# Token row loads on GpSimd, a tile's expert choice beside the context units, a buffer for the context, two gates ahead

## What is computed

```python
def peer_ffn(u, wq, k1, k2, eu, ev):              # for each chunk of 128 tokens
    q = (xc @ wq).reshape(PEER_CHUNK, PEER_HEADS, 2, half)
    v1, i1 = lax.top_k(s1, PEER_TOPK)             # s1, s2: scores against 2 x 128 keys per head
    v2, i2 = lax.top_k(s2, PEER_TOPK)
    cand = (v1[..., :, None] + v2[..., None, :]).reshape(PEER_CHUNK, PEER_HEADS, -1)
    top_s, pos = lax.top_k(cand, PEER_TOPK)
    g = jax.nn.softmax(top_s, -1)
    h = jax.nn.gelu(jnp.einsum('thkd,td->thk', eu[eidx], xc), approximate=False)
    return jnp.einsum('thk,thkd->td', g * h, ev[eidx])
```

## Time and profile before

| | before |
|---|---|
| median of 3 runs | 3122.6 us |
| profiled execution | 3111.5 us (span 3109.7 us) |
| busy: TensorE matmul | 2384.4 us, 77% |
| busy: VectorE | 1922.8 us, 62% |
| busy: ScalarE | 408.3 us, 13% |
| busy: GpSimd | 732.5 us, 24% |
| moved | 1029.87 MB, mean 331 GB/s |
| mean granted clock of TensorE | 0.786 |

### The profile page before, as it was taken

The page is one execution under the profiler, slowest core; times in us unless marked ns, Lnnn a source line. Parts: engine busy times, 40 slices in busy tenths (PEclk is TensorE's granted clock), DMA queues, the critical chain, the costliest instruction groups (busy, mean ns, idle before and its releaser), DMA issues.

```text
span 3109.7 us, 34657 instructions
## 1 busy us (share of the span) xinstructions
PE 2384.4 (77%) x11936; PEld 1287.6 (41%) x11936; DVE 1922.8 (62%) x6212; ACT 408.3 (13%) x1015; POOL 732.5 (24%) x779
## 2 busy tenths in 40 slices
PE   6989996597899968758878877676897656665555
PEld 5878892053456535324545542112786111121111
DVE  3689977757545465877754455554448855555555
ACT  2151120014200010012010010000421000000000
POOL 0000002332322222222222223331001333333332
PEclk8999996597899979768989986556998555566556
DMA  8618748798899989868999999998144989999997
GB/s 322 237 68 333 296 173 331 301 402 346 341 403 418 393 320 381 337 263 355 378 374 408 421 376 407 397 395 353 53 152 155 351 335 397 392 378 403 399 398 304
DMA packets 155376, 1029.87 MB, mean 331 GB/s; under 512 B 19136, under 2 KB 29888, under 8 KB 34496
## 3 DMA queue, kind: packets, MB, share of 16 engines
q0 software_dynamic: 110592, 805.36, 64.9%
q1 hardware_dynamic: 31648, 209.70, 17.3%
q10 hardware_dynamic: 12960, 12.59, 1.2%
HBM read 1018.66 MB, written 8.91 MB: 330 GB/s over the span
## 4 chain that ended last, share of the span: by engine, by line
PE 45%; DMA 26%; DVE 15%; POOL 5%; issue 4%; ACT 3%; ACTq 1%; SPq 0%; DVEq 0%; POOLq 0%
DMA ring<-in_peer_uv,eT 24%; PE PS L1233 12%; DVE ring L2253 7%; PE PS L901 6%; POOL ring L717 5%; PE PS L1252 4%; PE PS L817 4%; PE PS L998 4%; PE PS L971 2%; PE PS L908 2%; PE PS L1079 2%; PE PS L819 1%; PE PS L1170 1%; PE PS L928 1%; PE PS L1095 1%
## 5 line engine op out<-in xcount | busy, mean ns | idle before, releaser
L2253 DVE CUSTOM_DVE_ANT_0 ring<-ring,PS 128x512 f32<-128x512 f32 x1536 | 994.0, 684 | 831.9 <-PE PS L1252 491.8
L717 POOL DMA_INDIRECT ring<-in_peer_uv,eT x768 | 730.6, 951 | 2348.0 <-PE PS L1233 1431.4
L1252 PE MATMUL PS<-xr,onesb 3*128 3x512 bf16 x1536 | 548.1, 482 | 485.5 <-DVE hcol L2253 400.7
L1233 PE MATMUL PS<-ring,zcol 128*32 128x512 f32 x3072 | 573.5, 886 | 108.4 <-DVE zcol L2263 106.4
L1252 PEld LDWEIGHTS PS<-xr,onesb 3*128 3x128 bf16 x1536 | 108.1, 95 | 1049.9 <-DVE hcol L2253 569.9
L1233 PEld LDWEIGHTS PS<-ring,zcol 128*32 128x32 f32 x3072 | 102.6, 141 | 390.2 <-issue 213.7
L901 PE MATMUL PS<-uT,W 128*128 128x256 f32 x1024 | 245.2, 388 | 3.7 <-ACT mix L1373 3.7
L1623 ACT ACTIVATE ge<-hdot 128x4 f32<-128x4 f32 x192 | 39.5, 206 | 1435.4 <-DVE hdot L2258 1435.3
L901 PEld LDWEIGHTS PS<-uT,W 128*128 128x128 f32 x1024 | 190.3, 191 | 53.3 <-issue 24.0
L1696 DVE CUSTOM_DVE_ANT_0 ring<-ring 128x1024 f32<-128x1024 f32 x160 | 190.1, 1220 | 7.6 <-DMA ring<-in_w_rows 3.4
L817 PE MATMUL PS<-uT,W 128*128 128x256 f32 (+1 forms) x720 | 168.7, 388 | 17.8 <-ACT uT L1316 17.8
(11 more groups left out here) (289 smaller groups left out, 2156.6 us busy)
## 6 DMA issues: line engine op xcount, KB each, us to landing
ring<-in_w_rows SPq DMA_DIRECT2D x40, 1024.0 KB, 7.9
W<-in_w_in SPq DMA_DIRECT2D x30, 1024.0 KB, 9.3
W<-in_w_gate SPq DMA_DIRECT2D x16, 1408.0 KB, 8.0
W<-in_w_gate SPq DMA_DIRECT2D x16, 1280.0 KB, 8.9
W<-in_w_out SPq DMA_DIRECT2D x20, 1024.0 KB, 5.1
W<-in_w_gate SPq DMA_DIRECT2D x16, 1152.0 KB, 10.5
ring<-in_w_q SPq DMA_DIRECT2D x16, 1024.0 KB, 13.4
ring<-in_peer_uv,eT POOLq DMA_INDIRECT x768, 10.3
```

Source lines behind the costliest of these rows:

```text
L717: pool.indirect_dma_start(ring[:, slot, :], None, (peer_uv0, peer_uv1)[b.l], bass.IndirectOffsetOnAxis(eT[:, f % 2, t:t + 1], 0)).then_inc ...
L1233: last = T.matmul(PS[k * NR:(k + 1) * NR, (6 + h) * 512:(7 + h) * 512], zcol[:, g % 2, k, NR - 1 - at:2 * NR - 1 - at], ring[:, slot, D + ...
L1252: T.matmul(bank(x_bank(q, n) + h), onesb[p0:p0 + 3, :], xr[p0:p0 + 3, g % 2, h * 512:(h + 1) * 512], start=True, stop=True)\
L2253: V.tensor_tensor_reduce(out=u_half, in0=u_half, in1=bank(x_bank(q, n) + h), scale=1.0, scalar=0.0, op0=ALU.mult, op1=ALU.add, accum_out=h ...
```

## The change

Four edits. (1) x_rows is gone from ScalarE. GpSimd issues the four loads of a group in ask, behind its waits and in front of the group's first request. (2) The choice of experts for the second tile of the layer-0 latents leaves the end of BL0 and is done by VectorE between the units of FC0, as it was for BC0's second tile between those of FL1; its TILE_READY comes at the end of FC0's units. (3) KV0's modulated input gets a buffer of its own, uK, in mix; the latents' transposes come behind KV0's first unit, into banks 6, 7 and 0, 1, and ScalarE modulates them between KV0's units. (4) In BL0 and BC0 the first two gates (8 matmuls each) are issued inside the last attention jobs; their statistics for the convolution move from bank 2 to bank 4.

```diff
+BESIDE = {FC0: BL0, FL1: BC0}
...
+        uK = part(mix, 0, [KD, TOK])
...
@@ front (GpSimd's, TensorE's, ScalarE's, VectorE's part alike)
-                if r is FL1:
+                if r in BESIDE:
                     yield "sel"
                     yield TILE_READY
...
@@ back, apart (the same on every engine)
                     for q in range(LATE):
                         yield "late"
-                    for q in range(8):
-                        yield "sel"
-                    yield TILE_READY
+                    if b.early:
+                        for q in range(8):
+                            yield "sel"
+                        yield TILE_READY
                     yield "rows"
...
@@ GpSimd, ask(n)
                     pool.wait_ge(weighed, (whole - SLOTS) // GRP + 1)
                 if b.apart and n < SLOTS:
                     pool.wait_ge(a["wo"], a.at("wo", TT * KD + 16 + 2 * n + 2))
+                if n % GRP == 0:
+                    g = n // GRP
+                    if g % NR == 0:
+                        tile = f"xs{g // NR}"
+                        pool.wait_ge(a[tile], a.at(tile, 48))
+                    for k in range(GRP):
+                        pool.dma_start(xr[32 * k:32 * k + 3, g % 2, :].rearrange("q (h d) -> q h d", h=2),
+                                       xrows[f, g // NR, :, k, g % NR].rearrange("h q d -> q h d")).then_inc(xr_land[g % 2], 16)
                 t = token(n // GRP, n % GRP)
...
@@ TensorE, front(r)
-                u_ = uT
+                u_ = uK if r is KV0 else uT
...
-                yield from transposes(a, at_of["norm", r], r.tiles)
+                if r is FL0:
+                    for tt in r.tiles:
+                        yield "ln"
+                else:
+                    yield from transposes(a, at_of["norm", r], r.tiles)
...
                     last.then_inc(a["unit"], 1)
+                    if r is KV0 and n == 0:
+                        for _ in transposes(at_of["front", FL0], at_of["norm", FL0], FL0.tiles, (6, 0)):
+                            pass
                     yield "unit"
...
@@ TensorE, conv(a): banks 2 become 4
-                conv_mean(a, 2)
+                conv_mean(a, 4)
...
-            def gates(a):
+            def gate_half(slot, n, k0=0, k1=KD):
+                wg = W[:, slot, 0:TILE].rearrange("p (k b n) -> p k b n", k=KD, b=2)
+                for k in range(k0, k1):
+                    T.matmul(bank(2 + n % 4, 0, TOK), wg[:, k, n % 2, :], uT[:, k, :], start=(k == 0), stop=(k == KD - 1))
+
+            def gates(a, slot):
...
+                        if n >= 2:
+                            gate_half(slot, n, 0, KD // 2)
+                        yield "gate"
+                        if n >= 2:
+                            gate_half(slot, n, KD // 2, KD)
...
@@ TensorE, back(b), the loop over the jobs
                     if 2 <= n < len(JOBS) + 2:
                         transposed(n - 2)
+                    ahead = n - len(JOBS) - s
+                    if not b.early and 0 <= ahead < 2:
+                        if not ahead:
+                            begun.append(arrived())
+                        gate_half(begun[0], ahead)
                     if n >= 3:
                         values(n - 3)
...
@@ ScalarE, front(r)
+                    if r is KV0 and 1 <= n < 5:
+                        f_ = at_of["front", FL0]
+                        tt = (n - 1) // 2
+                        act.wait_ge(f_["xnT"], f_.at("xnT", tt + 1))
+                        for k in range(KD)[n % 2 == 0 and slice(KD // 2, KD) or slice(0, KD // 2)]:
+                            last = modulated(uT, l, FL0.s, tt, k, (6, 0)[tt], 0, 8)
+                        if n % 2 == 0:
+                            last.then_inc(f_["u_ready"], 1)
...
@@ ScalarE, experts()
-                        if n == 0:
-                            if q:
-                                act.wait_ge(xb_s, 2 * q * TOK)
-                            x_rows(0)
-                            x_rows(1)
                         if k == GRP - 1:
                             act.wait_ge(summed, q * NG + g + 1)
                             A(ge[:, g % 2, :], hdot[:, g % 2, :], ACT.Gelu).then_inc(gelu_s, 1)
-                            if g + 2 < NG:
-                                x_rows(g + 2)
...
@@ VectorE, front(r)
-                if r is FL1:
-                    second = second_selection()
+                b = BESIDE.get(r)
+                if b:
+                    second = second_selection(b, r)
...
@@ VectorE, apart(b, a)
-                yield from selection(a, 1, isel)
+                if b.early:
+                    yield from selection(a, 1, isel)
                 split(1)
```

More of the change, by code:

```diff
@@ L771, in norm, with transposes @@
                     yield "ln"
-            def transposes(a, normed, tiles=tuple(range(TT))):
+            def transposes(a, normed, tiles=tuple(range(TT)), at=(2, 4)):
                 for n, tt in enumerate(tiles):
@@ L776, in transposes @@
                     for k in range(KD):
-                        last = T.transpose(bank(2 + 2 * tt + k // 4, (k % 4) * P, (k % 4 + 1) * P),
+                        last = T.transpose(bank(at[tt] + k // 4, (k % 4) * P, (k % 4 + 1) * P),
                                            scratch[:, tt, k * P:(k + 1) * P], ident[:, :])
@@ L828, in front @@
                 pe.wait_ge(a["unit_act"], a.at("unit_act", na))
-                if r is FL1:
-                    b = at_of["back", BC0]
+                if r in BESIDE:
+                    b = at_of["back", BESIDE[r]]
                     pe.wait_ge(b["sel"], b.at("sel", TT))
@@ L1038, in apart @@
                 pe.wait_ge(a["sc_s"], a.at("sc_s", 8))
[L1039 to L1042, removed]
-                        T.transpose(bank(5, P, 2 * P), ts[:, :, :].rearrange("p h k -> p (h k)"), ident[:, :])\
-                            .then_inc(a["selT"], 1)
-                        pe.wait_ge(a["sel_s"], a.at("sel_s", 2 * TT))
-                    yield "sel"
-                yield TILE_READY
+                if b.early:
+                    for q in range(8):
+                        if q == 7:
+                            pe.wait_ge(a["sel"], a.at("sel", TT))
+                            T.transpose(bank(5, 0, P), isel[:, 0, :], ident[:, :])
+                            T.transpose(bank(5, P, 2 * P), ts[:, :, :].rearrange("p h k -> p (h k)"), ident[:, :])\
+                                .then_inc(a["selT"], 1)
+                            pe.wait_ge(a["sel_s"], a.at("sel_s", 2 * TT))
+                        yield "sel"
+                    yield TILE_READY
                 pe.wait_ge(a["xread"], a.at("xread", TT))
@@ L1117, in back @@
                     pe.wait_ge(a["ya"], a.at("ya", 1))
-                    yield from gates(a)
+                    yield from gates(a, begun[0])
                 pe.wait_ge(a["macc"], a.at("macc", KD))
@@ L1320, in front @@
                 a, l, s = at_of["front", r], r.l, r.s
-                yield from modulate(a, l, s, uT, 0, 8, r.tiles)
+                if r is FL0:
+                    for tt in r.tiles:
+                        yield "ln"
+                else:
+                    yield from modulate(a, l, s, uK if r is KV0 else uT, 0, 8, r.tiles)
                 dst_of = {"cv": lambda j: cv[:, j, :], "nq": lambda j: nq[:, j, :], "nk": lambda j: nkb[s][:, j, :],
@@ L1483, in apart @@
                     yield "late"
-                for q in range(8):
-                    if q == 7:
-                        chosen(b, a, 1, 5)
-                    yield "sel"
-                yield TILE_READY
+                if b.early:
+                    for q in range(8):
+                        if q == 7:
+                            chosen(b, a, 1, 5)
+                        yield "sel"
+                    yield TILE_READY
                 rows_out(1)
@@ L1788, in front @@
                 taken(len(r.units) - 1)
-                if r is FL1:
+                if b:
                     for _ in second:
                         pass
-                    weighted(at_of["back", BC0], 1)
+                    weighted(at_of["back", b], 1)
                     yield "sel"
@@ L2048, in back, with second_selection @@
                 yield from selection(a, 0, isel)
-            def second_selection():
-                a, f = at_of["back", BC0], at_of["front", FL1]
+            def second_selection(b, r):
+                a, f = at_of["back", b], at_of["front", r]
                 dve.wait_ge(f["xnT"], f.at("xnT", TT))
```

30 lines of the change are left out of this document (9 added, 21 removed).

## The result

The changed kernel takes 3191.53 us, the median of 4 runs (3186.68 to 3200.14), against 3119.57 us of the kernel before in the same session (4 runs): ratio 1.0243, 95% interval 1.0223 to 1.0262, so 72 us slower. The profiled execution took 3188.1 us (span 3186.3). In the rows PE is TensorE's matmuls, PEld its weight loads, DVE VectorE, ACT ScalarE and POOL GpSimd.

What follows compares the result with a forecast made beforehand. Full DMA engines, with under 2 us to spare, were taken to bound the pure token stretches; +63 - 15 - 5 - 8 + 0 = +35 us gave 3147 us profiled, 3158 as median, range 3085 to 3225.

Steps and rivals of the forecast that it cites:

- the loads' term: Token row loads on GpSimd in front of each group's requests lengthen the expert ring's loop: +63 us together.
- The price c: Time of one token row load on GpSimd with its gap, taken as 0.93 us, nearer to GpSimd's gather than ScalarE's issue.
- 18.9 + 4c: Ring loop length in us without any queue, four loads included; only what exceeds the transfers' 21.4 us lengthens a turn.
- rival A: GpSimd's loads are cheap (c up to 0.6) and hidden by the queue's 1.7 us; gains leave 3095 us; chance 0.33.
- The second figure for the spare time: In the pure token stretch, only 1.5 to 1.8 us of DMA work is left ahead of a burst's first request.
- 37 pure turns and 18 shared ones: Ring turns charged for the loads: 37 with tokens only, 45 us; 18 chain passes in stretches shared with weights, 18 us.
- Token-row waits removed, -15: Chain waits for token rows of 15.00 and 7.44 us, the first behind ScalarE's context stores; counted 10 and 5 us won.
- Second latent tile -8: Selection moved beside the context units; 20 tokens then run at the end at 2.67 instead of 3.1 us: -8 us.
- own buffer -5: Own context buffer: transposes and modulation between context and latent units, 7.0 us, go beside the units: -5 us.
- gates 0: Gates of 3.72 us ahead of two last jobs' value products: worth 0, at most 3 us for each of two blocks.
- C: Rival: GpSimd becomes the bound if a load costs 1.4 us or more; 3245 us or more; chance 0.06.
- The lock-out by VectorE's two-port mode: GpSimd's descriptor writing is locked out during it; selection stretches would lose 1.5 us per load hit; nothing added.

Runs made afterwards that it cites:

- Two loads: The kernel on ScalarE plus two spare token row loads per group on GpSimd in front of the requests, read by nobody: 3166.28 us, 1.0146.
- one load: The changed kernel with one twelve-row load per group instead of four, on GpSimd in front of the requests, with masked broadcasts and more stores: 3134.98 us, 1.0058.
- the memsets: The kernel on ScalarE plus five small GpSimd memsets in front of each group's requests, no DMA added: 3178.07 us, 1.0204.
- the kernel on ScalarE: The changed kernel with the token row loads put back on ScalarE, the other three edits kept: 3088.78 us, 0.9907.
- the kernel with the loads behind: The changed kernel with GpSimd issuing the next group's four token row loads behind a group's requests instead of in front: 3074.65 us, 0.9879.
- the one-load pair: The changed kernel with one twelve-row load per group instead of four, on ScalarE (3108.83 us, 0.9976) and on GpSimd behind the requests (3100.18 us, 0.9936).
- the kernel without the edit: The kernel on ScalarE with the second latent tile's selection put back at the end of the latents' part: 3112.99 us over 10 runs, 0.9993.
- the spare loads behind: The kernel on ScalarE plus four loads per group repeated on GpSimd behind the requests, into partitions nobody reads: 3117.53 us, 1.0010.

## Why the prediction was right on the sign, and where its terms were off

**Verdict and sum.** It forecast slower, 3158 us, in a range to 3225; measured are 3191.5, so +72 us where the sum had +35. Its direction rests on the loads' place in the loop, and that mechanism is shown: the same loads behind the requests cost nothing, and a delay of nearly the same length without any load costs nearly as much. The loop's turn grew, to 23.0 to 23.3 us where the prediction had 22.6. That the sum came out on the right side is luck all the same: it needed a load that was taken as too dear, as the next paragraph shows.

**The size of the loads' term, +63, measured 105 to 113.** Two numbers in it were wrong, in opposite directions. The price c was taken as 0.93 us from POOL's gather; it is 0.605 us, and four with their one gap are 2.67 us instead of 3.7. With that price the prediction's own formula, a loop of 18.9 + 4c against 21.4, gives 21.6 us, a turn 0.2 us longer. In its sum that is 7 us for 37 turns and 9 us for the 18 shared ones, less 28 us of gains: 3111 us, faster than before, as its rival A had it. So **the step that failed is "at 4c = 2.5 this reaches the 21.4 us that the transfers need; above it each turn grows by 4c - 2.5"**: there is no such spare time. Two loads, 1.56 us with the gap, already cost 75 us, one load, 0.94 us, costs 38 us, and in the turns of the last stream above between nothing and 0.9 us of the time put in front is hidden, not 2.5. The 18.9 us were built from the best value of each piece, above all 5.3 us for a request that finds nothing ahead of it plus three tokens, 13.3 us from the first request to the last landing. In the changed kernel this stretch is 14.15 us in the turn above, though little was left ahead of it: the DMA share is 0.75 to 0.81 from 2673 to 2675. The least landing in the whole changed kernel is 7.1 us, not the 5.3 to 5.5 that the prediction wanted to see; but with the memsets it is 5.4 us at nearly the same loss, so it decides nothing, and why it differs is open. The second figure for the spare time, 1.5 to 1.8 us from the least landings, was read from one stretch, 2800 to 3109, and one burst. Before, in another pure stretch, 2600 to 2800, the least is only 0.5 us above 5.3:

```profile
DMA to landing us min/median/max: 5.8/9.8/13.7
```

A DMA share of 1.00 was read as a floor that hides what lies beside it. It is no such floor: with two loads in front the share from 1900 to 2100 is still 0.98.

**How many turns.** 37 pure turns and 18 shared ones were counted. The last stream alone, 32 turns, lost 54.7 us against the kernel on ScalarE (787.4 against 732.7 us), 1.7 us a turn, and the two streams before it 43 us (first request of the last stream at 2398.9 against 2355.6). The six turns from 2377 to 2529, counted at nothing, are among those 32. They lost little, 4.6 us for the first 48 requests of the stream (157.0 against 152.5 us), and 1.0 us with the memsets in front: there counting nothing was nearly right. The other 26 lost 51.0 us, 2.0 a turn.

**Token-row waits removed, -15.** The term was read from chain pieces of 15.00 and 7.44 us, while TensorE never waited more than 8.2 us for rows. The kernel with the loads behind is 9 us faster than the one with ScalarE's by the ratios, 11 by the spans, and in the one-load pair it is 12. So a gain of about the forecast size is there in the one-load pair, while for the four loads the intervals of the two ratios overlap. In the changed kernel itself the long waits gave way to many short ones, 359.6 us in 153 waits; the kernel with the loads behind waits 307.2 us there (209.3 and 97.9) and is the fastest, so these waits cost little by themselves.

**Second latent tile -8, own buffer -5, gates 0.** Together -13 were forecast, and 21 to 29 measured. The gates are right at 0. The buffer made the first latent unit 6.2 us earlier, where 5 were forecast; with the gates it is worth 2 to 10 us. The tile is worth 12 to 27. Its term counted only that 20 tokens run at 2.67 instead of 3.1 us; it left out that TensorE's parts start while VectorE selects. That this is where the rest comes from is argued from the windows below, not tested. Windows of the kernel without the edit, then of the kernel on ScalarE:

```profile
470.00:900.00 430.00, 321.01 (x1462) 147.24 (x1462) 284.63 (x996) 80.45 (x185) 125.59 (x130) 0.77 0.89 355
```

```profile
470.00:900.00 430.00, 349.76 (x1657) 179.81 (x1657) 292.92 (x1024) 84.62 (x195) 125.08 (x133) 0.83 0.94 375
```

With about the same tokens (130 and 133 requests) PE does 195 more matmuls by 900 us, 29 us of busy time. The granted clock is higher too (0.83 against 0.77), and what that gives was not taken apart. Of these 29 us 15 are left when the last stream's first request goes out (2355.6 against 2371.0).

**Rivals.** C, POOL as the bound, is ruled out: it is busy 53 to 55 of 100 us in pure stretches. A had the right price for a load and the wrong consequence: c is below its 0.7, and the kernel is slower. The kernels with the loads behind the requests are what A describes. The Trainium skill, "DMA: Bandwidth & Descriptors", section "Issuing engines are not separate DMA queues", has the issuer change only issue time, usually a small thing; the runs agree for the change of issuer (9 us faster, within the intervals). But the issue time itself is not small where it stands in the loop: 2.67 us in front of each group's requests cost 113 us against the same loads behind. The lock-out by VectorE's two-port mode, which the prediction takes from the Trainium skill, "SBUF — State Buffer", section "Who interferes with whom", is not seen on the loads: the longest of 768 took 1022 ns; one request took 2207 ns, as one did before, 2456 ns. Nor does the slow request of the earlier trace rows bear it out: the operation beside it is a TENSOR_TENSOR, which by that section has no two-port mode and contends only with GpSimd's reads. What slowed it is open.

**Announced signs.** Right: the DMA share near 0.93, the 15 us piece of the chain gone, the build of layer 1 unchanged (2136.8 to 2376.9 us before, 2155.6 to 2398.9 after between the requests around it, 240 and 243 us). Wrong: the price of a load and the least landing; the turn is 23.0 us for the 22.6 announced.

**Left open.** The turns of the changed kernel are longer in the mean (23.0 to 23.3 us) than the one in the chain above (22.49). Why part of the delay is hidden in most turns, and why a smaller part of it is paid before the last stream (43 of the 98 us between the two spans, in 64 of the 96 turns), was not taken apart. Nor was the 32 us of the spare loads behind split between POOL's time and the queues. Gates, buffer and tile were taken out of the version with the loads behind in no run.

## What to carry to other kernels

In a loop that runs request, landing, use, free slot, request, anything issued between "slot free" and "request" is paid in each turn even when the DMA engines show a share of 1.00: here two thirds or more of it where nothing else ran, and two fifths over the whole kernel. Put what is needed later behind the requests. Don't build a loop's floor from the best value of each piece: read the turn, and assume no spare time unless a stretch shows it. When independent work is moved beside a selection, count what the other engine gets done in that time, not only the rate of the tokens.

## What was not expected of the hardware

A plain load of 6 KB on GpSimd took 0.605 us against 0.98 for a gather of 1 MB with 128 rows, and one of twelve rows 0.635, so in these two shapes its price hardly follows the rows. Plain loads stand back to back, while 0.30 us lies ahead of each gather. The loads moved to GpSimd made 24,576 packets more on its queue, 32 each; the page's line of the queue, with 110,592 packets and 805.36 MB before:

```profile
q0 software_dynamic: 135168, 810.20, 65.2%
```

Twelve-row broadcasts from one group of partitions kept PE busy for 102 us more than three-row ones from four groups, at the same mean of one.
